# Joining the high and low halves of the values in one stationary tile, in the projections' sliding-window attention

## What is computed

```python
proj = rms_norm(x, g_attn) @ w_in
sq, sk, sv, ... = split(proj)
qa, ka = rotary(rms_norm(sq)), rotary(rms_norm(sk))
s = einsum('bnqhgd,bnkhd->bnhgqk', qc, kb) * 64 ** -0.5      # kb, vb: previous chunk and own chunk
p = exp(s - m);  denom = sum(p) + exp(sink - m)
out_a = einsum('bnhgqk,bnkhd->bnqhgd', p / denom, vb)         # the value sums
...
x = x + concat(out_a, out_b, out_m) @ w_o                     # out_b: latent attention, out_m: memory
x = x + square(relu(rms_norm(x) @ w_ff1)) @ w_ff2
```

## Time and profile before

| | |
|---|---|
| three runs | 2166.9, 2167.49, 2167.51 us, median 2167.49 |
| span of the profiled execution, first to last instruction | 2165.3 us |
| what lies around the span (median less span) | 2.2 us |
| PE busy | 2108.8 us, 97% |
| DVE, ACT, POOL busy | 1430.8, 1036.5, 1091.3 us |
| one steady step of the projections | 22.93 us |

### The profile page before, as it was taken

How to read it: one execution, slowest core, us unless ns; L and a number is a source line. 1 busy time by engine, 2 the same in 40 slices (tenths; PEclk the granted TensorE clock), 3 DMA queues, 4 the chain that set the end, 5 groups by cost and what they waited for, 6 DMA issues and landing times. The chain is left out here.

```text
span 2165.3 us, 30816 instructions
## 1 busy us (share of the span) xinstructions
PE 2108.8 (97%) x9992; PEld 1741.3 (80%) x9992; DVE 1430.8 (66%) x2103; ACT 1036.5 (48%) x1863; POOL 1091.3 (50%) x892
## 2 busy tenths in 40 slices
PE   8999999899999999989999989999999999999999
PEld 6899999777777777768888878888888888888887
DVE  5788888977655656578676797666634644354463
ACT  6566666567767666644333443333323223222221
POOL 2566665635465766468556666566346710020220
PEclk9999999999999999999999999999999999999999
DMA  7133243687676666665444654444678762233363
GB/s 249 39 111 94 83 121 113 212 250 243 189 212 192 196 188 209 233 197 185 160 140 146 235 191 152 141 145 165 214 242 279 238 206 104 98 136 133 134 221 115
DMA packets 293440, 374.20 MB, mean 173 GB/s; under 512 B 27150, under 2 KB 187118, under 8 KB 291519
## 3 DMA queue, kind: packets, MB, share of 16 engines
q1 hardware_dynamic: 293310, 372.56, 53.3%
HBM read 247.28 MB, written 125.19 MB: 172 GB/s over the span
## 5 line engine op out<-in xcount | busy, mean ns | idle before, releaser
L128 PE MATMUL bank<-f_t_hi,f_w_hi 128*128 128x512 f32 x896 | 350.1, 391 | 14.5 <-DVE f_w_lo L1888 7.5
L128 PE MATMUL bank<-f_t_hi,f_w_lo 128*128 128x512 f32 x896 | 349.1, 390 | 0.0
L128 PE MATMUL bank<-f_t_lo,f_w_hi 128*128 128x512 f32 x896 | 349.1, 390 | 0.0
L128 PE MATMUL bank<-f_w_hi,f_a_hi 128*128 128x512 f32 x896 | 348.5, 389 | 0.0
L128 PE MATMUL bank<-f_w_lo,f_a_hi 128*128 128x512 f32 x896 | 348.5, 389 | 0.0
L128 PE MATMUL bank<-f_w_hi,f_a_lo 128*128 128x512 f32 x896 | 348.5, 389 | 0.0
L2727 POOL TENSOR_TENSOR a_p_lo<-a_prob,a_p_hi 128x512 fp32r<-128x512 f32 (+1 forms) x192 | 233.9, 1229 | 175.5 <-DVE a_p_hi L2872 65.6
L128 PEld LDWEIGHTS bank<-f_t_hi,f_w_hi 128*128 128x128 f32 x896 | 168.5, 188 | 52.8 <-issue 16.5
L2039 POOL TENSOR_TENSOR f_r<-f_r,f_y 128x512 f32<-128x512 f32 x24 | 42.1, 1787 | 325.3 <-DMA f_r<-s_x 325.3
L2140 DVE TENSOR_TENSOR f_a_lo<-f_a_raw,f_a_hi 128x1024 fp32r<-128x1024 f32 x112 | 157.5, 1406 | 73.4 <-ACT f_a_hi L2064 73.2
L128 PEld LDWEIGHTS bank<-f_t_hi,f_w_lo 128*128 128x128 f32 x896 | 168.5, 188 | 35.2
(11 more groups left out here) (340 smaller groups left out, 4832.7 us busy)
## 6 DMA issues: line engine op xcount, KB each, us to landing
f_a_raw<-s_aop SPq DMA_DIRECT2D x112, 512.0 KB, 4.4
w_raw<-in_w_ff SPq DMA_DIRECT2D x64, 512.0 KB, 5.3
s_aop<-f_a SPq DMA_DIRECT2D x128, 256.0 KB, 4.4
s_aop<-f_s SPq DMA_DIRECT2D x96, 256.0 KB, 2.4
f_w_raw<-in_w_ff SPq DMA_DIRECT2D x64, 256.0 KB, 5.7
f_t_raw<-s_hop SPq DMA_DIRECT2D x14, 1024.0 KB, 8.3
f_r<-in_w_ff SPq DMA_DIRECT2D x48, 256.0 KB, 6.2
a_vals<-s_v SPq DMA_DIRECT2D x40, 264.0 KB, 4.8
```

Of the source, the lines that this page charges most:

```text
L128: ins = pe.matmul(out, a, b, start=(first and j == 0), stop=(last and j == n - 1))
```

## The change

The values' high and low parts stand side by side: `v_own` and `v_mix` are [128, head, part, 64], so that one stationary tile is 128 wide and holds both parts. One matmul by `p_hi` and one by `p_lo` then give the high sums on partitions 0 to 63 of `pD` and the low sums on partitions 64 to 127 (the product low times low is computed too, which it was not before). That is 8 matmuls of 128x256 for a tile, not 12 of 64x256. ScalarE copies both halves out, into `mo` and a new `mo_lo`, in 4 instructions; GpSimd adds them (`sum_out`), at the end of its step; SP's store waits for that addition. The last three tiles keep the old form.

```diff
+        def joined(t):
+            return t.n < NT - 3
@@ SP
                 def store_mix(t):
-                    wait(sp, out_made, (t.n + 1) * 2)
+                    if joined(t):
+                        wait(sp, out_summed, t.n + 1)
+                    else:
+                        wait(sp, out_made, (t.n + 1) * 2)
@@ GpSimd
-                    st.link(pool.tensor_scalar(own[:, 0, :], proj[:, C_V:C_QA], 1.0, 1.0, ALU.mult, ALU.mult))
-                    st.link(pool.tensor_tensor(own[:, 1, :], proj[:, C_V:C_QA], own[:, 0, :].bitcast(F32), ALU.subtract))
+                    st.link(pool.tensor_scalar(own[:, :, 0:SD], new, 1.0, 1.0, ALU.mult, ALU.mult))
+                    st.link(pool.tensor_tensor(own[:, :, SD:], new, own[:, :, 0:SD].bitcast(F32), ALU.subtract))
...
+                def sum_out(t):
+                    wait(pool, out_made, (t.n + 1) * 2)
+                    pool.tensor_tensor(mo[t.b][:, :, :], mo[t.b][:, :, :], mo_lo[:, :, :], ALU.add).then_inc(out_summed, 1)
...
+                    t = tile_at(i, s - 3)
+                    if live(t, NT):
+
+                        sum_out(t)
                 steps(pool, body, drain, prepare, lambda: O["gpsimd_means"](pool))
@@ ScalarE
-                    src = pD[0:SD, :].rearrange("d (n k e q) -> d k n e q", n=2, k=HP, e=2)
+                    if joined(t):
+                        wait(ac, out_summed, t.n)
                     for e in range(2):
-                        ac.activation(mo[t.b][e * SD:(e + 1) * SD, :, :].rearrange("d k (n q) -> d k n q", n=2),
-                                      src[:, :, :, e, :], ACT.Copy).then_inc(out_made, 1)
+                        for part, dst in enumerate((mo[t.b], mo_lo) if joined(t) else (mo[t.b],)):
+                            src = pD[part * SD:(part + 1) * SD, :].rearrange("d (n k e q) -> d k n e q", n=2, k=HP, e=2)
+                            ins = ac.activation(dst[e * SD:(e + 1) * SD, :, :].rearrange("d k (n q) -> d k n q", n=2),
+                                                src[:, :, :, e, :], ACT.Copy)
+                        ins.then_inc(out_made, 1)
@@ TensorE, in score
                         if mixes:
-                            weigh_part(before, 2 * (b - ALONE_FIRST))
+                            weigh_joined(before, b - ALONE_FIRST + (b == NB8 - 1))
                         ins = pe.matmul(out, q, k_lo[t.b][:, g, pick, :], start=False, stop=True)
...
-                        if mixes:
-                            weigh_part(before, 2 * (b - ALONE_FIRST) + 1)
-                        else:
+                        if mixes and b >= NB8 - 2:
+                            weigh_joined(before, b - 1 if b < NB8 - 1 else b)
+                        elif not mixes:
                             up(t, b)
...
+                def weigh_joined(t, m):
+
+                    n, g, j = m // 4, m // 2 % 2, m % 2
+                    v, p = (v_mix if n == 0 else v_own)[t.b], (p_hi, p_lo)[j]
+                    cols = slice(g * SG * CHUNK, (g + 1) * SG * CHUNK)
+                    ins = pe.matmul(pD[:, n * SH * CHUNK + cols.start:n * SH * CHUNK + cols.stop],
+                                    v[:, g, :, :].rearrange("p e d -> p (e d)"), p[:, n, cols], start=j == 0, stop=j == 1)
```

More of the change, by code:

```diff
@@ L611, in front @@
         k_lo = [sb(f"k_lo{b}", [P, SKV, 3, CHUNK], F32R) for b in range(2)]
-        v_own = [sb(f"v_own{b}", [P, 2, SKV * SD], F32R) for b in range(2)]
-        v_mix = [sb(f"v_mix{b}", [P, 2, SKV * SD], F32R) for b in range(2)]
+        v_own = [sb(f"v_own{b}", [P, SKV, 2, SD], F32R) for b in range(2)]
+        v_mix = [sb(f"v_mix{b}", [P, SKV, 2, SD], F32R) for b in range(2)]
+        mo_lo = sb("mo_lo", [P, HP, P])
         tab_s = [sb(f"tab_s{b}", [P, ROPE_W]) for b in range(2)]
@@ L669, in front @@
         p_turned, p_hi_done, p_lo_done = sem("p_turned"), sem("p_hi_done"), sem("p_lo_done")
-        weighed, out_made = sem("weighed"), sem("out_made")
+        weighed, out_made, out_summed = sem("weighed"), sem("out_made"), sem("out_summed")
         m_stored, lv_stored, l_stored, mo_stored = (R["front_" + n] for n in ("m_stored", "lv_stored", "l_stored", "mo_stored"))
@@ L841, in _ @@
                 wait(pool, const_made, 7)
-                pool.memset(v_mix[0][CHUNK:, :, :].bitcast(F32), 0.0).then_inc(const_made, 1)
+                pool.memset(v_mix[0][CHUNK:, :, :, :].bitcast(F32), 0.0).then_inc(const_made, 1)
                 wait(pool, const_made, 8)
@@ L876, in split_values @@
                     own, mix, before = v_own[t.b], v_mix[t.b], v_own[1 - t.b]
-                    st.link(pool.tensor_scalar(own[:, 0, :], proj[:, C_V:C_QA], 1.0, 1.0, ALU.mult, ALU.mult))
-                    st.link(pool.tensor_tensor(own[:, 1, :], proj[:, C_V:C_QA], own[:, 0, :].bitcast(F32), ALU.subtract))
+                    new = proj[:, C_V:C_QA].rearrange("p (g d) -> p g d", g=SKV)
+                    own, mix, before = (x[:, :, :, :].rearrange("p g e d -> p g (e d)") for x in (own, mix, before))
+                    st.link(pool.tensor_scalar(own[:, :, 0:SD], new, 1.0, 1.0, ALU.mult, ALU.mult))
+                    st.link(pool.tensor_tensor(own[:, :, SD:], new, own[:, :, 0:SD].bitcast(F32), ALU.subtract))
                     st.link(pool.tensor_scalar(mix[0:CHUNK, :, :], own[0:CHUNK, :, :].bitcast(F32), 1.0, 1.0, ALU.mult, ALU.mult))
@@ L1527, in weigh_part @@
                     v, e, p = (v_mix if n == 0 else v_own)[t.b], (0, 0, 1)[j], (p_hi, p_lo, p_hi)[j]
-                    cols, feat = slice(g * SG * CHUNK, (g + 1) * SG * CHUNK), slice(g * SD, (g + 1) * SD)
-                    ins = pe.matmul(pD[0:SD, n * SH * CHUNK + cols.start:n * SH * CHUNK + cols.stop], v[:, e, feat], p[:, n, cols],
+                    cols = slice(g * SG * CHUNK, (g + 1) * SG * CHUNK)
+                    ins = pe.matmul(pD[0:SD, n * SH * CHUNK + cols.start:n * SH * CHUNK + cols.stop], v[:, g, e, :], p[:, n, cols],
                                     start=j == 0, stop=j == 2)
                     if m == 11:
+                        ins.then_inc(weighed, 1)
+                def weigh_joined(t, m):
+                    n, g, j = m // 4, m // 2 % 2, m % 2
+                    v, p = (v_mix if n == 0 else v_own)[t.b], (p_hi, p_lo)[j]
+                    cols = slice(g * SG * CHUNK, (g + 1) * SG * CHUNK)
+                    ins = pe.matmul(pD[:, n * SH * CHUNK + cols.start:n * SH * CHUNK + cols.stop],
+                                    v[:, g, :, :].rearrange("p e d -> p (e d)"), p[:, n, cols], start=j == 0, stop=j == 1)
+                    if m == 7:
                         ins.then_inc(weighed, 1)
```

## The result

The changed kernel takes 2172.03 us (median of 17 runs) against 2167.51 for the kernel before (17 runs): ratio 1.0021, 95% interval 1.0015 to 1.0028, +4.5 us. Predicted were 2171.0 us and +3.5. The profiled execution has a span of 2168.5 us and took 2170.26 in all; its span is 3.2 us longer than that of the kernel before, so what follows explains this pair of traces and not the last microsecond of the medians.

The account below looks back on a forecast made before the run. PE, busy 97% of the span, was taken to bound the joined tiles, and DVE the drain. 1.4 (PE) + 1.25 (held rotation) + 0.8 (late load) = 3.45 us on 2167.5 gave 2171.0 us, range 2166.0 to 2175.5.

Parts of the forecast that it names:

- PE in the joined tiles: Value matmuls of blocks 2 to 7: 2.27 us instead of 2.16 a tile, +1.4 us over 13 tiles.
- Rival A: Joined tiles: loads hide and matmuls cost their moving columns alone, 6.2 us go from PE, time 2163.3; chance 0.10.
- One of my signs to look for: PE's timeline in the joined tiles: a k_hi matmul and the value matmul behind it 0.11 us apart, not 0.06.
- ACT in the joined tiles: Two more copies cost 1.20 us, the 1.00 wait at L981 covers all but 0.2, which ends nothing: cost 0.
- POOL and SP in the joined tiles: Steady steps: POOL's addition of 1.29 us and SP's stores and loads about 6 us later, each at cost 0.
- The drain, first part: Last step: POOL's addition holds DVE's rotation of the latents, and all DVE work behind it, 1.25 us longer.
- The drain, second part: SP's store of `mo` waits 7.0 us longer, e_x lands late, DVE waits 0.8 us (0 to 1.6).
- rival C: Drain costs another 2 to 3 us by later loads, e_swa blocking ACT or a lost PE clock, about 2174; chance 0.17.
- rival B: Drain hides its part: addition falls beside a gap, e_x lands in time, 1.4 us left, 2168.9; chance 0.20.
- The sum: Whole kernel: 1.4 (PE) + 1.25 and 0.8 (drain) = 3.45 us, nothing after the drain, 2171.0 us.

Follow-up runs that it names:

- the swap: Changed kernel, but VectorE makes the latents' low half ahead of the low half of x; 2171.04 us, ratio 1.0016 to the kernel before.

## Why the prediction was right, and where it was not

**PE in the joined tiles:** right. 2.27 us predicted and measured; the runs put it at 0.12 us a step (23.05 against 22.93), and 1.4 us in 13 tiles, as said, since the last of them counts for half. The rule of the longer of columns and load, read from the earlier trace rows, then gave 2.75 and 1.88 for two other orders, where 2.76 and 1.90 were measured. The Trainium skill, "TensorE: Matmul & The Clock Gate", section "LDWEIGHTS (loading the stationary operand)", has 64 columns more cost an estimated 53 ns; the run with 12 wide matmuls agrees, (2.76 - 2.16) / 12 = 0.050 us. Rival A falls with it: four matmuls fewer pay 0.26 us a tile, but widening the other eight takes 0.38. One of my signs to look for was wrong: the records show the value matmul 0.05 us behind k_hi, not 0.11, and k_lo 0.18 behind the value matmul; only the sum and the loads' starts tell.

**ACT in the joined tiles: this is the step that failed.** The prediction said of the 0.2 us that went on past the wait of the earlier trace rows: "It ends nothing", cost 0, with the low probabilities as the only margin looked at. Its sign came true (L998, the new number of L981, starts at 221.36 without a wait), but the cover of 1.00 us at L981 was not what protects GpSimd: its mean square needs the square of x, which stands ahead of L981. In the kernel before the square's sum was there at 219.89 and GpSimd started at 220.93; after, it starts 0.16 us behind that sum. So the cover was 0.9 us for copies of 1.2, and what was over went into GpSimd's time, then VectorE's. And the nearest consumer was another one: TensorE began the transposes into `pC` 0.12 us after the latents' low half was there (225.38, first load at 225.50), while I looked at a margin of 0.65 us. Measured cost: 0.09 us a step, 1.1 us up to the scores of tile 14 (316.65 against 315.54), taken away by the swap (23.14 to 23.05). With the narrow matmuls 0.25 us more of ScalarE's time produce 0.14 (22.92 to 23.06).

**POOL and SP in the joined tiles:** right. The addition takes 1.31 us against 1.29, and costs nothing there: with the swap and the addition in its place the step is 23.05, as in the kernel without any addition.

**The drain, first part:** right in size. The rotation is held 1.13 us longer against 1.25, and with the load in time (the store of tile 12 late) the addition into `e_x` comes 1.07 later.

**The drain, second part:** the mechanism right, the size not. SP's store comes 7.0 us later than its place, as said, but e_x(0) was issued at 406.04 and landed 6.0 us later, where I took the median of before, 4.9; the wait was 2.11 against 0.8 (0 to 1.6). In three other traces with the same late store it was 1.6 to 2.9. Then the clock, which the sum has at nothing, added 1.15 us. Late loads and a lost clock are what rival C names. Some 1.4 us come back before the attention stage begins (+6.67 to +5.23): PE is idle for 2.8 us of that stretch and not 3.8. So much of rival B holds.

**The sum.** 3.45 us was predicted and 4.5 measured. From the first scores to those of tile 15 the parts are 2.3 (1.4 of PE and 1.1 of ACT, less 0.2 for one step that took 23.13 us in the kernel before), 1.1 (the rotation), 2.1 (the load) and 1.15 (the clock), 6.7 in all. Against that, 1.4 came back in the drain and 1.1 from the attention on, where nothing is changed; the cause of that last one stays open, and single executions of one kernel spread over 5 us. So it is partly luck that the time came out near: the missing 1.1 of ACT and the 2.3 by which the drain cost more met 2.6 that came back and that I had not counted.

## What to carry to other kernels

Before joining small matmuls into wider ones, price each by the longer of its own moving columns and the load that follows: matmuls of 128 columns hide a stationary tile of 64 columns and not one of 128. When an engine that has idle time gets more work, don't ask only where its next wait is: list for each thing made behind the new work who wants it and how soon, since the smallest of these margins decides, and a swap on the way there may cost nothing. A wait put into a queue that issues loads delays all of them; in the steady steps here that cost nothing, in the last step it did. And where TensorE waits longer, look at its granted clock behind the wait as well.

## What the runs showed of the hardware

The distance between ScalarE's copies of 64x512 from PSUM is not always the same. Where a copy reads and writes the same partitions as the one ahead of it, it starts 0.48 to 0.50 us behind it; where source or target changes to the other half, 0.59 to 0.62 us (the kernels with 12 narrow matmuls and four copies). Two kernels show it, and the quick copies read the very same values again, so whether partitions or addresses decide is not shown.

A matmul whose load is late has a recorded start from which its price can't be read: the value matmul stands at 211.19, its load of 128 columns started at 211.14, and the next matmul comes 0.18 later where a value matmul with a narrow tile has 0.12. Its record is also longer, 0.33 us against 0.28. Whether the start is recorded too early or the matmul starts and is held isn't shown. Sums over a few matmuls came out right by the rule, single distances did not.

TensorE's granted clock differs from kernel to kernel at the same place of the program, 0.50 to 1.00 behind the first addition into `e_x`. Matmuls of 512 columns are 0.43 us apart there at 0.50 and 0.23 at 1.00, and the stretch took 4.95 to 6.67 us.
